# GpSimd's low halves of weights: two instructions of 512 elements for a quarter in place of four of 256

## The reference

```python
# first block, two layers: a spatial gating unit and differential attention side by side,
# then a feed-forward of 2816 channels with a width-3 convolution
def diff_attention(q, k, v, positions, lq1, lk1, lq2, lk2, subln_g, layer_idx):
    q = q.reshape(B, S, N_HEADS, 2, HEAD_DIM)
    ...
# second block: a gated linear recurrence and a compressed / selected / window attention,
# then a squared-ReLU feed-forward of 4096 channels: h = relu(x @ w_ff1) ** 2 ; y = h @ w_ff2
# every dense product is x @ W in float32: W (1024 x 1024 and wider) is read once from HBM
```

## Time and profile before

| | us |
|---|---|
| time, median of 3 runs | 1813.84 |
| lowest and highest of them | 1811.12, 1815.26 |
| span of the profiled execution | 1809.1 |
| busy in the span: PE, DVE, ACT, POOL | 1770.8, 1123.6, 780.7, 987.3 |
| TensorE's granted clock by stretch | 0.98 to 1.00 of full speed |

### The profile page before, as it was taken

How to read it: one execution, slowest core, us unless ns; L and a number is a source line. 1 busy time by engine, 2 the same in 40 slices (tenths; PEclk the granted TensorE clock), 3 DMA queues, 4 the chain that set the end, 5 groups by cost and what they waited for, 6 DMA issues and landing times. The chain is left out here.

```text
span 1809.1 us, 26088 instructions
## 1 busy us (share of the span) xinstructions
PE 1770.8 (98%) x9009; PEld 1440.2 (80%) x9009; DVE 1123.6 (62%) x1862; ACT 780.7 (43%) x1270; POOL 987.3 (55%) x1228
## 2 busy tenths in 40 slices
PE   8999999999999999999999999999999989999998
PEld 6867888888888886788888888877666778899886
DVE  4777656566656338756666655654486567666665
ACT  5434543333334334443333333456576664333332
POOL 6543445555465543255465564447311558888885
PEclk9999999999999999999999999999999999999999
DMA  7221224443423221122443332413201112223321
GB/s 255 94 94 47 82 75 158 151 147 120 151 93 117 93 93 48 47 105 105 151 162 123 134 125 93 140 50 109 101 2 48 47 47 94 93 95 115 117 94 47
DMA packets 102183, 183.73 MB, mean 102 GB/s; under 512 B 6810, under 2 KB 66892, under 8 KB 100044
## 3 DMA queue, kind: packets, MB, share of 16 engines
q1 hardware_dynamic: 101916, 182.46, 28.7%
q10 hardware_dynamic: 176, 0.07, 0.0%
HBM read 180.42 MB, written 2.10 MB: 101 GB/s over the span
## 5 line engine op out<-in xcount | busy, mean ns | idle before, releaser
L979 POOL TENSOR_TENSOR w_lo<-raw,w_hi 128x256 fp32r<-128x256 f32 (+1 forms) x1124 | 909.8, 843 | 796.6 <-ACT w_hi L1048 793.0
L2460 PE MATMUL ps<-n_hi,w_hi 128*128 128x512 f32 (+1 forms) x1320 | 509.0, 386 | 3.9 <-ACT zc L1351 1.8
L2462 PE MATMUL ps<-n_hi,w_lo 128*128 128x512 f32 (+1 forms) x1320 | 499.7, 379 | 0.0
L2461 PE MATMUL ps<-n_lo,w_hi 128*128 128x512 f32 (+1 forms) x1320 | 499.1, 378 | 0.0
L1048 ACT ACTIVATE w_hi<-raw 128x1024 fp32r<-128x1024 f32 (+2 forms) x331 | 307.7, 937 | 353.1 <-PE ps L2462 235.9
L2460 PEld LDWEIGHTS ps<-n_hi,w_hi 128*128 128x128 f32 x1320 | 248.1, 188 | 54.2 <-issue 7.2
L2461 PEld LDWEIGHTS ps<-n_lo,w_hi 128*128 128x128 f32 x1320 | 248.3, 188 | 47.3 <-issue 2.6
L2462 PEld LDWEIGHTS ps<-n_hi,w_lo 128*128 128x128 f32 x1320 | 247.9, 188 | 47.7
L2004 DVE TENSOR_TENSOR ps<-ps,sq 128x512 f32<-128x512 f32 x88 | 61.3, 699 | 181.3 <-PE ps L2462 178.9
L2460 PE MATMUL ps<-x_hi,w_hi 128*128 128x512 f32 x416 | 167.2, 402 | 0.1
L2462 PE MATMUL ps<-x_hi,w_lo 128*128 128x512 f32 x416 | 162.2, 390 | 0.0
(11 more groups left out here) (357 smaller groups left out, 2639.5 us busy)
## 6 DMA issues: line engine op xcount, KB each, us to landing
raw<-in_w_up SPq DMA_DIRECT2D x44, 1024.0 KB, 6.6
raw<-in_w_ff SPq DMA_DIRECT2D x32, 1024.0 KB, 6.5
raw<-in_w_in SPq DMA_DIRECT2D x26, 1024.0 KB, 6.1
zb<-in_ada_w SPq DMA_DIRECT2D x16, 1536.0 KB, 8.2
raw<-in_w_down SPq DMA_DIRECT2D x44, 512.0 KB, 4.2
raw<-in_w_out SPq DMA_DIRECT2D x12, 1024.0 KB, 6.5
raw<-in_w_in SPq DMA_DIRECT2D x4, 512.0 KB, 8.1
za<-in_x SPq DMA_DIRECT2D x4, 512.0 KB, 6.0
```

The costliest lines, as they stand in the source:

```text
L979: last = pool.tensor_tensor(part[0], part[1], part[2], ALU.subtract)
L2460: pe.matmul(out, l_hi, r_hi, start=start, stop=False)
L2461: pe.matmul(out, l_hi, r_lo, start=False, stop=False)
L2462: return pe.matmul(out, l_lo, r_hi, start=False, stop=stop)
```

## The change

`LO_PARTS` goes from 4 to 2. A quarter of 1024 elements is then subtracted by two GpSimd instructions of 512 elements each in place of four of 256. For H stripes the slices become the two rows of 512 of the view. In `gains_and_weights` the pieces at each of the four places are one instruction in place of two. The D2 quarters have two parts before and after. All line numbers behind L972 go down by one.

```diff
-LO_PARTS = 4
+LO_PARTS = 2
...
                 for i in range(pieces[0], min(pieces[-1] + 1, LO_PARTS if st.kind == "H" else count)):
                     if st.kind == "H":
-                        c = (i // 2, slice(i % 2 * 256, i % 2 * 256 + 256))
-                        part = [v[:, c[0], c[1]] for v in parts]
+                        part = [v[:, i, :] for v in parts]
                     else:
...
                 row_gains(0, 3)
-                lo(g, g + 1, g - 3, range(0, 2))
+                lo(g, g + 1, g - 3, range(0, 1))
                 row_gains(3, 5)
-                lo(g, g + 1, g - 3, range(2, 4))
+                lo(g, g + 1, g - 3, range(1, 2))
                 row_gains(5, 6)
-                lo(g + 1, g + 2, g - 2, range(0, 2))
+                lo(g + 1, g + 2, g - 2, range(0, 1))
                 row_gains(6, 8)
                 pool.wait_ge(rows_set, 2 * NT)
-                lo(g + 1, g + 2, g - 2, range(2, 4))
+                lo(g + 1, g + 2, g - 2, range(1, 2))
```

## The result

The changed kernel takes 1829.33 us (median of 5 runs, 1826.57 to 1830.04), the kernel before 1811.12 us (5 runs, 1810.21 to 1815.26). The ratio is 1.0087, 95% interval 1.0070 to 1.0103: slower by about 16 us (the two medians are 18.2 us apart; each ratio here is against runs of the kernel before that were taken beside it, and their medians go from 1811.12 to 1815.80 us). 1825.8 was forecast, in a range of 1813 to 1832.

The account below looks back on a forecast made before the run. TensorE was taken as the bound, busy 1770.8 of 1809.1 us. Terms 8.2 + 3.1 + 2.0 + 1.5 − 2.85 = +11.95 gave a span of 1821, with 4.7 outside it 1825.8 us; range 1813 to 1832.

Parts of the forecast that it names:

- What an instruction costs: GpSimd: 0.14 us less for each of 510 instructions removed, some 70 us; VectorE's pace beside pieces 1.08 to about 1.64.
- Seven-product stage: Six iterations: late x_lo delay TensorE's q4 and q5, 0.7 us in the first, 1.5 in five others, sum +8.2 us.
- The step most in doubt: Seven-product stage: VectorE's L2357 goes between q5's two GpSimd pieces; it depends on half a microsecond of timing.
- First block's attention: VectorE instructions meeting longer GpSimd pieces make TensorE late: 1.57 us a layer, +3.1 for two, bounds 0 and 4.5.
- the one worked example: First block's attention, pieces from 156.53: three VectorE instructions get through later, TensorE's L2670 at 165.20 has no slack, +0.73 us.
- Gains: TensorE's idle time caused by GpSimd's late chains of quarters shrinks at five places: −2.85 us, bounds −3 and −1.5.
- three places of the same kind: First block: places where a chain of GpSimd quarters runs behind, forecast to gain −0.5, −0.4 and −0.35 us.
- Second block's attention and output: VectorE held up beside GpSimd's pieces: +2.0 us (bounds 0 to 3) and, around L2252, +1.5 (bounds 0 to 2).
- The 4.7 us outside the span: Profiled span of the kernel before is 4.7 us below its runs' median, 1813.84; the same was added to the forecast span.
- (a): Rival, faster: GpSimd done sooner, w_lo of q4 within its 0.27 us slack; 4.7 us gained, 1809.2; chance 0.07.
- (b): Rival, no change: slack takes up half of VectorE's delay, 8.2 becomes 1.8, attention terms halve; +2.2, 1816; chance 0.15.
- (c): Rival, slower still: late x_lo goes whole into q4, again into q5 and q6, 17.4 for 8.2; 1835; chance 0.08.

Follow-up runs that it names:

- m1: Separate kernel without the reference's computation: VectorE instructions beside GpSimd pieces of one width; VectorE takes 0.61 us alone, 1.14 beside 256, 1.68 beside 512.
- e3: Changed kernel with ScalarE's high part of q4 issued ahead of its wait for the x_lo; 1816.43 us, ratio 1.0012 to the kernel before.
- e4: Kernel before with two pieces only for q4 and q5 of the six seven-product stripes; 1810.59 us, ratio 0.9988.
- e9: Kernel before with two pieces for one attention quarter in each layer, q3 of outs; one run, 1816.76 us.
- e6: Kernel before with two pieces only for the first four quarters of each layer's up matrix; 1815.15 us, ratio 1.0008.
- e7: Kernel before, two pieces for S q3 to q5, first quarters of second layer and g_rnn, last ff2 stripe; q4's high part before x_lo wait; 1807.78 us.
- e11: As e7, but with quarters 247 to 249 in two pieces in place of the first of g_rnn; 1806.89 us, ratio 0.9948 to the kernel before.
- e1: Kernel before with two pieces only from the first seven-product stripe to the end; 1818.44 us, ratio 1.0032.
- e10: As e7, but with quarters 250 to 253 in two pieces in place of the first of g_rnn alone; 1808.04 us, ratio 0.9971 to the kernel before.
- e8: Kernel before with one wait more: VectorE's L2357 waits until GpSimd has ended q5's low part; 1811.49 us, ratio 0.9995.
- e2: Kernel before with two pieces only ahead of the first seven-product stripe, four from there on; 1821.76 us, ratio 1.0046.
- e5: Kernel before with eight pieces of 128 where the view allows, not S stripes or down; 1829.68 us, ratio 1.0089.

## Why the prediction was right, and where its terms were off

The mechanism was right: VectorE and GpSimd take turns, and the late `x_lo` reach TensorE through ScalarE's queue. It carried the larger part of the result. Point by point, in the order of the sum:

**What an instruction costs.** Forecast 1.26 us for 512 alone and a turn of 1.64 beside it. Measured 1.23 and 1.68 in m1, and 1.69 for `x_lo` in the kernel (6.54 / 4 = 1.64 in the iteration shown). GpSimd's busy time fell by 105 us, not 70: 0.14 us for each of 510 instructions is the part alone. That the rest are turns in which it waited for VectorE, fewer now, fits m1 but was not counted.

**Seven-product stage.** Forecast −0.3, +1.1 and +0.7, in sum +1.5 an iteration; measured −0.36, +1.35, +0.61 and −0.07 behind them = +1.53 in five, +0.8 in the first (0.7 forecast), +8.4 in all for 8.2. e3 and e4 show the path: slow `x_lo`, L1601, `w_hi` of q4. The step most in doubt, L2357 between q5's pieces, came true.

**First block's attention.** Forecast +3.1 for two layers. Measured +0.95 −0.10 +0.43 +0.75 +0.16 = +2.2 in the first, +1.6 by the same places in the second (+0.39, −0.17, +0.42, +0.79, +0.19), 3.8 in all. e9 has the one worked example within 0.06 us; the first term, +0.4, came in the second layer and was +0.95 in the first (at 114 us); why is not known.

**Gains.** Forecast −2.85. Three of the five came: −0.63 at 582.40, −1.37 at 1247.68, −0.47 at 1787.43, −2.5 for the −1.9 of them. This is where the sum failed: "−0.5, −0.4 and −0.35 at three places of the same kind" took the stalls at 218.65 and 790.68 for GpSimd's alone. The same quarters also have VectorE's norm chain beside them, and the changed kernel has +0.14 at 218.65, +0.54 at 226.93, nothing at 790.68 and +0.52 at 798.95 in place of −0.9. e6 shows the 1.0 us at 226.93 and 798.95 with those quarters alone. A further +0.4 at 1166.78 was not foreseen, and no run asked for it.

**Second block's attention and output.** Forecast +3.5. Measured from 1320 to 1421: +0.65, −0.08, +0.89, +0.69, +0.17, +0.56 = +2.9 for 2.0; the step at 1395.27 had been left out. Before L3105 it was +0.83 at 1448.36 and +0.53 at 1454.65, +1.4 for 1.5. Directly behind it the changed kernel loses another 1.5 us that is none of VectorE's: the granted clock is 0.50 there, and it was 1.00 before. In turn it lacks a fall of the clock at 1285 us, −1.5 (last section). The two nearly cancel, and with −1.4 at 1247.68 the stretch shows +2.6.

**The clock.** The prediction had nothing to be had or lost there, since the granted clock is 0.98 to 1.00 in every stretch. Read in windows of 100 us it is, and a fall of 3.4 us hardly shows in one of them. The profiled execution of the kernel before had such a fall, that of the changed kernel one of 6.8 us. No term stood for them, and that the two cost about the same in these two executions is luck.

**The time.** The span came out 15.6 us up for 11.95, 1824.7 for 1821. The 4.7 us outside the span were wrong too: the profiled execution of the changed kernel has 1826.57 us for a span of 1824.7, 1.9 us outside it. The median of its runs is 2.8 us above that execution, which no term had; it goes with the clock, whose mean over the run is 0.997 there and 0.994 or 0.995 in the four others. The two errors in the base nearly cancel by luck, and 1825.8 is 3.5 below 1829.33, about what the sum itself lacks.

**The rivals.** (a) needed `w_lo` of q4 within its 0.27 us; q4 started 1.35 us late. e7 shows the stage that (a) describes, with q3 early and q4 not late: −0.28 at each of six q3. (b) needed VectorE's delay to be absorbed: in the seven-product stage none was. (c) is excluded by q6, which has no step.

The Trainium skill's rule of the shared port pair (page "SBUF — State Buffer", section "Who interferes with whom") holds in m1 in three points. With two SBUF inputs VectorE contends with GpSimd (1.68 us for 0.61). With at most one, outside the modes that use both ports, it does not (0.61 with a PSUM operand). `tensor_scalar` can enter such a mode and can contend (1.41 beside 512; alone it was not measured).

## What to carry to other kernels

The length of an instruction on GpSimd is the price that VectorE pays for meeting it. Pieces of 512 for 256 save 0.14 us for each instruction less on GpSimd and cost 0.54 us (1.68 for 1.14) for each VectorE instruction of two SBUF operands that meets one, so the number of pieces is best chosen by place: long where VectorE is quiet and the low part is late, short where a chain through VectorE ends in a wait. Before lengthening, follow what is queued behind the waiting engine; in the changed kernel one line's move in ScalarE's queue was worth 11.8 us.

## What the runs showed of the hardware that was not expected

The granted clock falls for a short stretch in some executions. In the profiled one of the kernel before it was 0.50, TensorE's 1.2 GHz level, from 1284.3 to 1287.7 us, after 4.5 us in which TensorE was busy for 3.0 (a wait of 1.5 us at 1282.15 and small matmuls), and 1.00 in the same stretch of the changed kernel. Windows of before, then of the changed kernel (busy us by engine, clock, DMA share, GB/s):

```profile
1280.00:1284.50 4.50, 3.00 (x22) 2.06 (x21) 1.31 (x3) 3.34 (x5) 0.00 (x0) 0.98 0.00 0
1284.50:1287.50 3.00, 3.00 (x9) 2.35 (x8) 0.00 (x0) 2.15 (x5) 1.42 (x3) 0.50 0.00 0
```

```profile
1283.50:1288.00 4.50, 3.16 (x24) 2.23 (x22) 1.34 (x3) 3.32 (x5) 0.00 (x0) 1.00 0.00 0
1288.00:1291.00 3.00, 3.00 (x25) 2.33 (x23) 0.00 (x0) 2.19 (x5) 1.39 (x2) 1.00 0.00 0
```

It costs 1.5 us (the step of −1.5 between 1284 and 1288 where it is missing: the changed kernel, e6, e11). The traces of e1 to e4 and e7 to e10 have the fall at the same place in the program, with GpSimd's pieces there cut in two or in four; e8 and e10 have one more near 1162 us (+1.4).

The changed kernel has its fall later, while TensorE multiplies by the diagonals of L3104: 24 matmuls take 5.43 us for 3.27. Before it fell, TensorE was busy for 3.0 of 7.3 us. TensorE before, then TensorE and the windows in the changed kernel:

```profile
1454.65 3.27 PE L3105 MATMUL ps<-ss,zb 128*128 128x128 f32 x24 [0.81 <-DVE ss L2252]
```

```profile
1460.85 5.43 PE L3104 MATMUL ps<-ss,zb 128*128 128x128 f32 x24 [1.23 <-DVE ss L2251]
...
1452.00:1459.30 7.30, 3.00 (x24) 2.81 (x24) 7.03 (x14) 4.86 (x15) 2.29 (x2) 1.00 0.00 1
1459.30:1466.00 6.70, 5.47 (x27) 5.17 (x26) 4.23 (x10) 4.58 (x10) 1.26 (x1) 0.50 0.01 2
```

VectorE makes their start 0.53 us later than it was in the kernel before, and behind them TensorE is 2.0 us later, so the fall costs 1.5. e2 and e3, which have two pieces there as well, fall at the same place for as long and at 1427 us too (+1.6 in their stretch to 1500); e1, e6 to e11 with four do not. e4, also with four, has one at 1452.5 without a lasting loss, and e5 with eight one at 1461.8. Whether the waits for VectorE that the change makes longer bring the fall about is not shown. What decides in which execution the clock falls is not shown either.

An order between two engines that nothing fixes is not the same in every trace: one code of the stage, in kernels that differ ahead of it, let L2357 in among q5's pieces in 1, 3, 5 or 6 of six iterations, at 0.8 us each.
